# Second transformer block of a two-block fp32 kernel: activations kept by features, squares summed by one-column matmuls

## The reference

```python
for l in range(2):
    mod = silu(c) @ ada_w[l] + ada_b[l]            # shift, scale and gate (1024 each) of three sublayers
    h = rmsnorm(x, ffn1_norm[l]) * (1 + sc1) + sh1
    x = x + 0.5 * gt1 * ((silu(a) * b) @ ffn1_w_out[l])      # a, b = split(h @ ffn1_w_in[l]), 2816 each
    h = rmsnorm(x, mix_norm[l]) * (1 + sc2) + sh2
    x = x + gt2 * (mixers(h @ mix_w_in[l]) @ mix_w_out[l])   # attention, causal convolution, gated linear attention
    ...                                                      # ffn2 as ffn1, with sh3, sc3, gt3
```

## Time and profile before

| | us |
|---|---|
| median of 3 runs | 3317.07 (3315.16 to 3328.78) |
| the profiled execution | 3321.86 |
| its span | 3320.1 |
| TensorE busy in it | 3137.9 |
| VectorE, ScalarE, GpSimd busy | 1988.0, 972.5, 635.6 |

### The profile page before, as it was taken

How to read it: one execution, slowest core, us unless ns; L and a number is a source line. 1 busy time by engine, 2 the same in 40 slices (tenths; PEclk the granted TensorE clock), 3 DMA queues, 4 the chain that set the end, 5 groups by cost and what they waited for, 6 DMA issues and landing times.

```text
span 3320.1 us, 45976 instructions
## 1 busy us (share of the span) xinstructions
PE 3137.9 (95%) x18020; PEld 2698.3 (81%) x18020; DVE 1988.0 (60%) x1814; ACT 972.5 (29%) x985; POOL 635.6 (19%) x628
## 2 busy tenths in 40 slices
PE   7999989999989999899998899899889999999899
PEld 3888879978868888688877698798878979888797
DVE  6654366657277433774338766675686656567644
ACT  1212122212122121211214343333533333343342
POOL 0210100114111010110101022122561202237020
PEclk9999999999999999899999999999989999999999
DMA  7533334322344333353333477586446859754464
GB/s 272 177 127 89 101 105 164 113 89 77 102 135 157 114 89 122 106 164 102 101 117 115 165 238 257 157 271 220 158 165 181 275 166 281 231 178 154 124 187 157
DMA packets 501035, 523.22 MB, mean 158 GB/s; under 512 B 15652, under 2 KB 432726, under 8 KB 500886
## 3 DMA queue, kind: packets, MB, share of 16 engines
q1 hardware_dynamic: 497720, 513.76, 48.2%
q0 software_dynamic: 3168, 7.36, 1.1%
HBM read 520.01 MB, written 1.05 MB: 157 GB/s over the span
## 4 chain that ended last, share of the span: by engine, by line
PE 80%; DVE 10%; ACT 3%; POOL 3%; issue 2%; DMA 2%; SPq 0%; DVEq 0%; ACTq 0%; POOLq 0%
PE ps L1730 43%; PE ps L1801 22%; PE ps L1770 7%; DVE wl L1034 2%; PE ps L1680 1%; ACT wh L708 1%; POOL wst L678 1%; PE ps L1716 1%; DVE x L1130 1%; PE ps L1833 1%; DMA wraw<-in_ffn_w_in 1%; POOL lnp L684 1%; ACT ptmp L739 1%; PE ps L1698 1%; DVE st L1157 1%
## 5 line engine op out<-in xcount | busy, mean ns | idle before, releaser
L1034 DVE TENSOR_TENSOR wl<-wraw,wh 128x2048 fp32r<-128x2048 f32 x341 | 852.6, 2501 | 685.2 <-ACT wh L708 678.2
L1730 PE MATMUL ps<-xh,wh 128*128 128x256 f32 (+1 forms) x3008 | 994.3, 331 | 23.1 <-DVE xl L1086 19.7
L1730 PE MATMUL ps<-xl,wh 128*128 128x256 f32 (+1 forms) x3008 | 989.3, 329 | 0.0
L1730 PE MATMUL ps<-xh,wl 128*128 128x256 f32 (+1 forms) x3008 | 989.2, 329 | 0.0
L708 ACT ACTIVATE wh<-wraw 128x2048 fp32r<-128x2048 f32 x341 | 652.3, 1913 | 617.2 <-PE ps L1801 574.6
L1730 PEld LDWEIGHTS ps<-xh,wh 128*128 128x128 f32 x3008 | 568.4, 189 | 84.7 <-issue 25.5
L1730 PEld LDWEIGHTS ps<-xl,wh 128*128 128x128 f32 x3008 | 568.0, 189 | 58.5
L1730 PEld LDWEIGHTS ps<-xh,wl 128*128 128x128 f32 x3008 | 568.3, 189 | 57.3
L1011 DVE SCALAR_TENSOR_TENSOR acc<-mraw,svec,acc 128x1024 f32<-128x1024 f32 x329 | 426.7, 1319 | 20.5 <-DMA mraw<-in_w_mod 7.9
L1801 PE MATMUL ps<-wh,hh 128*128 128x512 f32 x968 | 383.2, 396 | 1.7 <-DVE wl L1034 1.7
L1801 PE MATMUL ps<-wh,hl 128*128 128x512 f32 x968 | 382.9, 396 | 0.0
(11 more groups left out here) (338 smaller groups left out, 3057.4 us busy)
## 6 DMA issues: line engine op xcount, KB each, us to landing
wraw<-in_ffn_w_in SPq DMA_DIRECT2D x352, 512.0 KB, 5.1
wraw<-in_ffn_w_out SPq DMA_DIRECT2D x176, 512.0 KB, 4.2
mraw<-in_ada_w SPq DMA_DIRECT2D x72, 1024.0 KB, 7.6
mraw<-in_w_mod SPq DMA_DIRECT2D x64, 1024.0 KB, 5.4
wraw<-in_gmlp_w_in SPq DMA_DIRECT2D x48, 512.0 KB, 4.4
wraw<-in_mix_w_in SPq DMA_DIRECT2D x48, 512.0 KB, 4.7
wraw<-in_gmlp_w_out SPq DMA_DIRECT2D x24, 512.0 KB, 4.2
first_w<-in_w_mod SPq DMA_DIRECT2D x8, 1024.0 KB, 13.4
```

The source lines that it names most:

```text
L1034: dve.tensor_tensor(wl[:, slot], wraw[:, slot], wh[:, slot].bitcast(F32), ALU.subtract)\
L1730: m = pe.matmul(ps[:, bank, 0:width], a, b, start=k == p == 0, stop=k == KD - 1 and p == 2)
```

## The change

In the second block x is kept transposed (xT, in the place of x[:, 0]): eight chunks of 128 features, 256 tokens each. The output stage makes y by features too (weights stationary, hh and hl moving, 256 columns, one chunk after another), and the gate is then a number per partition, made by columns like shift and scale.

- **Passage.** VectorE takes a chunk of y as its output is done (take_chunk); ScalarE makes the high half and a square of it, GpSimd three of the eight squares, VectorE the low half (low_chunk). TensorE starts unit 0 chunk by chunk. The 16 blocks of squares (8 chunks by 2 token tiles) go straight into 16 one-column matmuls; nothing adds them first. gate_rows, the transposes and keep_going are gone within the block.
- **Feed-forward.** The matmuls run on x times gain and scale without the token's factor; the shift rides along as two more moving columns (XW = 258). The factor is spread by two matmuls (rows_of_factors) in the middle of unit 1 and copied to SBUF, and VectorE multiplies it to both halves of every unit's result, ahead of silu, and adds the shift's part (evac).
- **Mixer.** The factor is needed first: squares, factor, then chunks, then unit 0.
- The mod_unit calls stand at the units of FF_MODS (before at 0, 2, 4, ... 14, 16, 17, 19, 21), the mixer's tables and the gains are loaded one sublayer earlier. Loops of the second block's feed-forward are written out. Sublayer 6 is entered by enter() after 16 transposes; the end transposes xT back and writes four parts.

```diff
+XW = T + 2
...
+FF_MODS = (2, 4, 6, 8, 10, 12, 14, 16, 18, 20, 22, 23)
+FF_COLUMNS = (9, 17)
+NATURAL, MIXED = tuple(range(8)), (0, 1, 4, 5, 6, 7, 2, 3)
...
+        xT = x[:, 0].rearrange("p t d -> p (t d)").rearrange("p (k q) -> p k q", k=KD)
+        sq = lnp_flat.rearrange("p (k q) -> p k q", k=KD)
+        rstd_b = rope[:].rearrange("p t a d -> p (t a d)")
...
             for s in subs:
+                nxt = after(s)
                 if s["block"] == 2:
+                    if s["kind"] == "ffn":
+                        for n in range(5, 8):
+                            j = order_in(s)[n]
+                            pool.wait_ge(xt_ready, 8 * s["m"] + n + 1)
+                            pool.tensor_tensor(sq[:, j], xT[:, j], xT[:, j], ALU.mult).then_inc(sq_pool, 1)
                     power()
...
+                if nxt and nxt["block"] == 2:
+                    if nxt["i"] > B2:
+                        pool.wait_ge(gain_used, nxt["i"] - B2)
...
+                    if nxt["kind"] == "mix":
+                        mix_tables(nxt)
...
+            def arrive(s):
+
+                pre, shift = prea[:, 0], modc[:, s["i"] % 2, 0, 0]
+                act.wait_ge(x_mod, s["i"] + 1)
+                if s["kind"] == "mix":
+                    for n, j in enumerate(order_in(s)):
+                        act.wait_ge(xt_ready, 8 * s["m"] + n + 1)
+                        act.activation(sq[:, j], xT[:, j], ACT.Square).then_inc(sq_act, 1)
+                    for n, j in enumerate(order_in(s)):
+                        act.wait_ge(t_ready, s["n_mix"] * 8 + n + 1)
+                        act.activation(xh2[:, j, 0:T], sq[:, j], ACT.Identity, bias=shift[:, j:j + 1]).then_inc(hi_ready, 1)
+                    return
+                act.activation(xh2[:, :, T:XW], shift.unsqueeze(2).broadcast_to([P, KD, XW - T]), ACT.Copy).then_inc(hi_ready, 1)
+                for n, j in enumerate(order_in(s)):
+                    act.wait_ge(xt_ready, 8 * s["m"] + n + 1)
+                    act.activation(xh2[:, j, 0:T], xT[:, j], ACT.Copy, scale=pre[:, j:j + 1]).then_inc(hi_ready, 1)
+                    if n < 5:
+                        act.activation(sq[:, j], xT[:, j], ACT.Square).then_inc(sq_act, 1)
+
             for s in subs:
...
+                if s["kind"] == "ffn" and s["block"] == 2:
+                    u0, q0 = s["n_unit"], s["n_inq"]
+                    for i in range(33):
+                        if u0 + i + 1 < u_end:
+                            split_next(u0 + i)
+                        if i == 0:
+                            act.wait_ge(rb_ps, s["m"] + 1)
+                            act.activation(rstd_b, ps[:, 6, 0:T], ACT.Copy).then_inc(rb_ready, 1)
+                        if i < KF:
+                            pair = i % 2
+                            act.wait_ge(a_ready, s["n_sg"] - subs[B2]["n_sg"] + i + 1)
+                            act.wait_ge(pair_free, q0 + i)
+                            act.activation(sg[:, pair, T:2 * T], sg[:, pair, 0:T], ACT.Silu, bias=shift_col[:, pair, 0:1])\
+                                .then_inc(sg_ready, 1)
...
+            def take_chunk(s, n):
+
+                j = s["order"][n]
+                per = 2 if s["kind"] == "mix" else 1
+                if n // per < 8 // per - 1:
+                    dve.wait_ge(y_tile, s["n_tile"] + n // per + 1)
+                else:
+                    dve.wait_ge(w_used, s["n_unit"] + (16 if s["kind"] == "mix" else 33))
+                y = ps[:, 4 + j // 2, j % 2 * T:j % 2 * T + T] if s["kind"] == "mix" else ps[:, j, 0:T]
+                dve.scalar_tensor_tensor(out=xT[:, j], in0=y, scalar=modc[:, s["i"] % 2, 2, 0, j:j + 1], in1=xT[:, j],
+                                         op0=ALU.mult, op1=ALU.add).then_inc(xt_ready, 1)
+
...
+            def low_chunk(s, n):
+
+                j = order_in(s)[n]
+                if s["kind"] == "mix":
+                    dve.wait_ge(hi_ready, s["n_hi"] + n + 1)
+                    src, by, op = sq[:, j], modc[:, s["i"] % 2, 0, 0, j:j + 1], ALU.add
+                else:
+                    dve.wait_ge(hi_ready, s["n_hi"] + n + 2)
+                    src, by, op = xT[:, j], prea[:, 0, j:j + 1], ALU.mult
+                dve.scalar_tensor_tensor(out=xl2[:, j, 0:T], in0=src, scalar=by, in1=xh2[:, j, 0:T].bitcast(F32),
+                                         op0=op, op1=ALU.subtract).then_inc(lo_ready, 1)
+
+            def mean_square(s):
+
+                dve.wait_ge(ss_ready, s["m"] + 1)
+                bank = 0 if s["kind"] == "mix" else 7
+                dve.tensor_scalar(rstd[:], ps[:, bank, 0:TT], 1.0 / D, RMS_EPS, ALU.mult, ALU.add).then_inc(var_ready, 1)
...
+            def arrive(s, nxt):
+
+                take_chunk(s, 0)
+                take_chunk(s, 1)
+                if nxt is None:
+                    for n in range(2, 8):
+                        take_chunk(s, n)
+                    return
+                if nxt["kind"] == "ffn":
+                    low_shift(nxt)
+                split_next(nxt["n_unit"] - 1)
+                if nxt["kind"] == "ffn":
+                    for n in range(8):
+                        if n + 2 < 8:
+                            take_chunk(s, n + 2)
+                        low_chunk(nxt, n)
+                    return
+                for n in range(2, 8):
+                    take_chunk(s, n)
+                mean_square(nxt)
+                dve.wait_ge(rb_ps, nxt["m"] + 1)
+                for n in range(9):
+                    if n < 8:
+                        j = NATURAL[n]
+                        dve.scalar_tensor_tensor(out=sq[:, j], in0=xT[:, j], scalar=prea[:, 0, j:j + 1], in1=ps[:, 6, 0:T],
+                                                 op0=ALU.mult, op1=ALU.mult).then_inc(t_ready, 1)
+                    if n:
+                        low_chunk(nxt, n - 1)
+
...
+                    def evac(i):
+                        pair = i % 2
+                        dve.wait_ge(w_used, u0 + i + 1)
+                        m = steps.mark(dve.tensor_copy(shift_col[:, pair], ps[:, 2 * pair:2 * pair + 2, T]))
+                        dve.tensor_tensor(sg[:, pair, 0:T], ps[:, 2 * pair, 0:T], rstd_b, ALU.mult).then_inc(a_ready, 1)
+                        m = steps.mark(dve.tensor_tensor(ht[:, pair, T:2 * T], ps[:, 2 * pair + 1, 0:T], rstd_b, ALU.mult))
+                        dve.wait_ge(sg_ready, s["n_sg"] + i + 1)
+
+                        dve.wait_ge(h_ready, s["n_h"] + i)
+                        steps.wait(m)
+                        dve.scalar_tensor_tensor(out=ht[:, pair, 0:T], in0=ht[:, pair, T:2 * T], scalar=shift_col[:, pair, 1:2],
+                                                 in1=sg[:, pair, T:2 * T], op0=ALU.add, op1=ALU.mult).then_inc(pair_free, 1)
+
+                    for i in range(33):
+                        if i < 32:
+                            split_next(u0 + i)
+                        if i == 0:
+                            mean_square(s)
+                            dve.wait_ge(rb_ready, s["n_sqp"] // 3 + 1)
...
+                        if nxt:
+                            for n, at in enumerate(FF_COLUMNS):
+                                if i == at + 1:
+                                    mod_end(nxt, n)
+                            if i == 26:
+                                mod_end(nxt, 2, 0, 384)
+                            for sec, q in ff_mods(i):
+                                mod_unit(nxt, sec, q)
+                        if i < KF:
+                            evac(i)
+                        if i == FF_COLUMNS[1] + 2 and nxt:
+                            factors(nxt)
...
+            def rows_of_factors(s):
+
+                pe.wait_ge(rstd_ready, s["rms_power"])
+                for t in range(TT):
+                    m = pe.matmul(ps[:, 6, t * P:(t + 1) * P], rstd[:, t:t + 1].broadcast_to([P, P]), ident[:], start=True, stop=True)
+                m.then_inc(rb_ps, 1)
...
+                if s["kind"] == "ffn" and s["block"] == 2:
+                    u0, q0, order = s["n_unit"], s["n_inq"], order_in(s)
+
+                    def squares_over_features():
+
+                        pe.wait_ge(sq_act, s["n_sqa"] + 5)
+                        pe.wait_ge(sq_pool, s["n_sqp"] + 3)
+                        for t in range(TT):
+                            for c in range(KD):
+                                m = pe.matmul(ps[:, 7, t:t + 1], sq[:, c, t * P:(t + 1) * P], ones[:, 0:1], start=c == 0, stop=c == KD - 1)
+                        m.then_inc(ss_ready, 1)
+
+                    for i in range(KF):
+                        slot, pair = (u0 + i) % 2, i % 2
+                        pe.wait_ge(wlo_done, u0 + i + 2)
+                        pe.wait_ge(pair_free, q0 + i)
+                        for r in range(2):
+                            for n, k in enumerate(order):
+                                if i == r == 0:
```

(39 more changed lines are left out.)

266 lines of the change are left out of this document (181 added, 85 removed).

## The result

The changed kernel takes 3357.34 us (median of 4 runs, 3354.33 to 3370.31), the kernel before 3316.51 in the same runs; the ratio is 1.012, 95% interval 1.009 to 1.015. It is slower by 1.2%, where the forecast was 3337 (0.6%) and the range 3310 to 3360. The sign held; the size was twice what the sum gave, and the reason for that is not one of the rivals.

A forecast was written before the change was run, and what follows sets the result against it. TensorE, busy 95% of the span, was taken as the bound. Losses of 40.0 (feature stage), 0.9 (width), 5.0 (gate columns) and 4.0 (clock), less 29.7 saved in passages, gave 20.2 over the 3317.07 median: 3337 us, range 3310 to 3360.

The forecast's parts named there:

- the ring: Feature stages of 6, 8, 9: VectorE and ScalarE alternate without overlap, 13.0 per pair against TensorE's 11.3; 40.0 us lost.
- Part 2: The feature stage gets longer: 40.0 us lost in sublayers 6, 8 and 9, 0.9 in the last sublayer.
- Output units keep their price: Output stages: matmuls of 256 columns cost no more than before; only the gate's columns add 3 x 1.68 = 5.0 us.
- Part 1: Passages get shorter: saved 4.6, 6.6 and 14.4 between sublayers, 3.1 into the block, 1.0 at the end; 29.7 us.
- the question between row and page: Feed-forward inputs: 32 one-column matmul instructions take 3.36 us by the trace row, 0.8 by the skill page's floor; row chosen.
- may run unit 0 at half rate here and still be in time: Mixer inputs: a slower TensorE in unit 0 costs nothing, as it waits for cgl from 17.5 to 20.6.
- 258 columns: Last sublayer's feature stage: two columns more than 256 make it 0.9 us longer over 20 units, between none and 3.
- The clock: Four feed-forward inputs: half-idle stretches and a 3 us wait lower the granted clock; 4.0 us lost, between 0 and 20.
- B: Rival: in the feature stage the ring is shorter than TensorE's pair, only the width is lost; 3297 to 3312, chance 0.10.
- C: Rival: the ring is real but at its short end, 12.6, and passages save a little more; 3312 to 3326, chance 0.17.
- E: Rival: in the feature stage each wl meets GpSimd and takes 2.83, 30 us more; 3367, chance 0.10.
- D: Rival: clock stays lower from unit 0 to unit 1 at all four feed-forward inputs, some 5 each; 3350 to 3360, chance 0.13.

The follow-up runs named there:

- e2: Changed kernel with mod_unit placed behind evac instead of ahead of it on VectorE: 3370.12 us, ratio 1.015 to the kernel before.
- e5: Changed kernel with mod_unit cut into two single steps, placed behind evac: 3377.49 us, ratio 1.019 to the kernel before.
- e1: Changed kernel with the gate columns copied on VectorE one unit earlier (25 instead of 26): 3342.65 us, ratio 1.007 to the kernel before.
- e10: e9 with the 16 blocks of squares on TensorE again, as in the changed kernel, nothing added first: 3303.79 us, ratio 0.996 to the kernel before.
- e9: Changed kernel with e1's copy, e3's order, squares added on VectorE, mod_unit in single steps, the last eight spread, mod loads and gate columns later: 3293.34 us, ratio 0.994.
- e8: Changed kernel with the edits of e1, e3 and e5, squares added on VectorE, and 256 moving columns instead of 258 (shift's part omitted): 3325.47 us, ratio 1.002.
- e12: e9 with the squares' sums taken earlier and the inputs' rows 1088 bytes apart instead of 1032: 3288.42 us, ratio 0.991 to the kernel before.
- e3: Changed kernel with unit 2's weight halves made ahead of the factors' copy and first silu: 3342.84 us, ratio 1.007 to the kernel before.

## Why the prediction was right, and where it was not

**What bounds the kernel; the ring (Part 2).** Right in sign, place and mechanism. TensorE waits 0.35 to 1.4 before every second unit from unit 6 on, but for those behind the columns, releaser VectorE, in sublayers 6, 8 and 9 and nowhere in 11; wh starts behind silu, silu behind VectorE. The term was 40.0 and measured 33.9, since a round takes 5.09 and not 5.26, and a pair 12.7 instead of 13.0; each unit waits less than the 1.4 to 2 I gave. Its picture as an average over two units was too kind, as e2 shows, but for the order that the change has, both pictures give the same. Not all of the 33.9 is the ring: in sublayer 6 the same stretch without its waits (e5) took 120.3, so 7.6 of the 11.4 is the ring, and the other 3.9 is the units of 5.76 instead of 5.60 (3.2) and the lower clock behind the wait before unit 2.

**The output stage.** This is the step that failed. "Output units keep their price" and "5.0 lost" for the gate's columns took TensorE's 1.68 and left out the wait for their copy on VectorE. It cost 13.7 of waiting and 5.8 of clock, which e1 took back in these stages (16.6 in the block). I had asked of each moved step what it costs, and not, of this one, who waits for the step that comes after it and what is queued ahead of that. With it the sum is 20 + 19.5 = 39.7, and the measured 40.8 lies close; but that is partly luck. By the table the passages came out 11.1 dearer than forecast and sublayer 11 5.4, and against that stand 6.1 of the ring, 4.6 of the mixers and the 4.0 of the clock, which cancel them but for 1.8.

**The passages (Part 1).** The feed-forward inputs were right: the forecast's 4.6, 2.8 and 3.8 saved came out at 3.9, 2.0 and 4.4, with a wait of 2.81 before unit 2 where 3 was forecast, and the 16 squares at 3.46 where 3.36 was. The last of these decides the question between row and page that I had posed, and the row was right: by the Trainium skill's floor ("TensorE: Matmul & The Clock Gate", section "Wait — 56ns, not 53.3ns?") 32 rows would take about 0.8; they took 3.46, 108 ns each, so the floor is not what binds here, and e10 against e9 shows that most of this time lies on the path (8.4 of 12 by the four inputs). The mixers' inputs saved 4.1 and 4.0 instead of 7.2: unit 1 came 21.1 after the end of the last output unit, not 17.8. VectorE's first product came 5.8 after that end where 3.9 was counted, since the last squares ended at 3.5 and not 2.2, and the mean, the power and the two spreading matmuls took 2.3 and not 1.7. VectorE's 16 steps took 6.9 where 7.2 was counted. The gate's matmuls took 4.54 where 2.81 was counted: that is the lower clock, and half of the miss. My "may run unit 0 at half rate here and still be in time" held for unit 0, which ended 1.9 before cgl (the low half that the gate's matmuls wait for) was ready; I had not asked the same of the 24 matmuls behind it, which nothing hides. Into the block nothing was saved: TensorE's columns of the gate and the filler there took 3.3 and 5.6, transposes came late, and the whole start ran at 0.78 of the clock.

**258 columns.** 0.9 was forecast, 5.9 measured, of which 3.2 is 20 units of 5.76 instead of 5.60 and the rest the lower clock of 0.69 in the first 10 us. e8 excludes the width for three quarters of the 0.16, and e12 shows that a larger distance of the rows does not help. What it is stays open; the rows' distance of before, the order of the loops and the waits in them are what is left to try.

**The clock.** 4.0 was forecast. The runs show 5.8 in the output stages (e1), 2.8 in sublayer 11 (e3) and 3.1 in the mixers' inputs (the gate's matmuls at 4.54 and 4.53, against 3.0 in the other runs), 11.7 in all. I had looked for it in the feed-forward inputs alone.

**The rivals.** B (no ring) is out. C's pair, 12.6, is in fact nearer to the 12.7 measured than the forecast's 13.0; its time is out because of the output stages and the passages. E is out: wl took 2.31 on average in the feature stage, with hl (0.83 on average) mostly done when it starts. The measured time falls into D's interval (3350 to 3360), but D's mechanism is not what put it there: the granted clock was 0.92, 0.92 and 0.99 in the last three feed-forward inputs, and 0.78 only in the first. That the range held is partly luck: it reached to 3360 for D's sake, and what filled it was a wait that stood in no rival.

## What to carry to other kernels

When a step is moved, follow the step that hands its result on as well: look at what stands ahead of that in its engine's order and at what can't start before it; here one index (26 for 25) cost 17 to 20 us. With two buffers an engine's latency must fit into each single step of the consumer, and slack of one step doesn't help the next; small steps laid one into each gap beat pairs of them, once the loads that wait for them are moved too (e5 against e9). And a test of the clock has to look where the slow stretch lies: filler gains nothing where TensorE has time in hand anyway. Last, an in-order DMA queue with loads for several users stops for the slowest of them, so a load goes into it only when its slot is already free.

## What the runs showed of the hardware

- A one-column fp32 matmul over 128 rows costs 108 ns for each of its two instructions when 16 stand in a row (3.46 / 32), nearly what 256 columns cost (117 to 120).
- GpSimd's subtraction of 128 x 256 took 0.74 alone and 2.61 when it started 0.3 after VectorE's 128 x 2048 subtraction, which kept 2.29 (e5). When GpSimd's started 0.8 earlier, as in e2, VectorE's took 2.83.
- A wait of 4.55 on TensorE was followed by a granted clock of 0.72 from 2294 to 2300; without the wait (e1) it stayed at 1.00. The same 24 matmuls at a mixer's entry took 4.54 where the granted clock had fallen (0.62) and 2.96 to 3.01 where it had not.
- The first block's time, in the same code, differed by up to 20 us between profiles, and the medians of the kernel before by 4 us between the groups of runs. A difference of 10 us between two traces can be nothing.
